# Stick-breaking attention: the causal mask added in the score banks by the tensor engine, every tile weighed by the vector engine alone

## The reference, cut to what matters

```
z = einsum(q_blk, k_pre) * scale                       # 128 queries x (i+1)*128 keys
strict = k_pos[None, :] < q_pos[:, None]
log_rest = where(strict, log_sigmoid(-z), 0.0)
suffix = cumsum(log_rest, reverse=True) - log_rest
a = where(strict, exp(log_sigmoid(z) + suffix), 0.0)
out = einsum(a, v_pre)
```

## Time and profile before

| what | value |
|---|---|
| median of three runs | 2162.31 us |
| the profiled execution: time, span | 2162.35 us, 2160.6 us |
| PE, DVE, ACT, POOL busy over the span | 93%, 66%, 42%, 33% |
| stick-breaking stage | about 898 to 1085 us |
| mean granted PE clock | 0.965 |

### The profile page before, as it was taken

How to read it: one execution, slowest core, us unless ns; L and a number is a source line. 1 busy time by engine, 2 the same in 40 slices (tenths; PEclk the granted TensorE clock), 3 DMA queues, 4 the chain that set the end, 5 groups by cost and what they waited for, 6 DMA issues and landing times. The chain is left out here.

```text
span 2160.6 us, 26117 instructions
## 1 busy us (share of the span) xinstructions
PE 2015.9 (93%) x9585; PEld 1679.5 (78%) x9585; DVE 1428.6 (66%) x1921; ACT 904.2 (42%) x1606; POOL 723.4 (33%) x602
## 2 busy tenths in 40 slices
PE   4899999999999999877889999994999999999997
PEld 3688888887887689666778888883888888887886
DVE  7756556559798532599955565567656565569896
ACT  6443443434445212566633444443443433334443
POOL 3655545530003021388711100124645555520000
PEclk7899999999999999899899999996999999999999
DMA  3222223244300221432134432230223222264201
GB/s 118 73 83 69 88 83 93 78 179 170 138 20 6 87 89 59 108 78 59 48 91 126 136 88 59 60 108 0 79 83 93 79 82 87 75 239 151 78 1 79
DMA packets 217496, 190.21 MB, mean 88 GB/s; under 512 B 7532, under 2 KB 173976, under 8 KB 217368
## 3 DMA queue, kind: packets, MB, share of 16 engines
q1 hardware_dynamic: 217280, 188.51, 28.2%
q10 hardware_dynamic: 88, 0.02, 0.0%
HBM read 152.85 MB, written 35.65 MB: 87 GB/s over the span
## 5 line engine op out<-in xcount | busy, mean ns | idle before, releaser
L1731 DVE TENSOR_TENSOR w_lo<-st,w_hi 128x512 fp32r<-128x512 f32 x176 | 192.7, 1095 | 200.6 <-ACT w_hi L1321 200.4
L928 PE MATMUL ps<-T_hi,w_lo 128*128 128x512 f32 x704 | 278.4, 395 | 48.4 <-DVE T_lo L1731 47.7
L929 PE MATMUL ps<-T_lo,w_hi 128*128 128x512 f32 x704 | 276.6, 393 | 0.0
L930 PE MATMUL ps<-T_hi,w_hi 128*128 128x512 f32 x704 | 276.4, 393 | 0.0
L928 PE MATMUL ps<-tr_hi,sr_lo 128*128 128x512 f32 x616 | 242.6, 394 | 5.1 <-DVE xT L1920 2.7
L930 PE MATMUL ps<-tr_hi,sr_hi 128*128 128x512 f32 x616 | 240.5, 390 | 0.0
L929 PE MATMUL ps<-tr_lo,sr_hi 128*128 128x512 f32 x616 | 240.3, 390 | 0.0
L928 PE MATMUL ps<-B_hi,w_lo 128*128 128x512 f32 x528 | 207.7, 393 | 8.5 <-DVE w_lo L1731 6.1
L929 PE MATMUL ps<-B_lo,w_hi 128*128 128x512 f32 x528 | 207.3, 393 | 0.0
L930 PE MATMUL ps<-B_hi,w_hi 128*128 128x512 f32 x528 | 207.1, 392 | 0.0
L928 PEld LDWEIGHTS ps<-T_hi,w_lo 128*128 128x128 f32 x704 | 133.6, 190 | 82.6 <-DVE T_lo L1731 33.9
(11 more groups left out here) (236 smaller groups left out, 4752.5 us busy)
## 6 DMA issues: line engine op xcount, KB each, us to landing
gate_raw<-in_ffn_w_gate SPq DMA_DIRECT2D x44, 512.0 KB, 5.3
up_raw<-in_ffn_w_up SPq DMA_DIRECT2D x44, 512.0 KB, 5.1
h_spill<-up_s SPq DMA_DIRECT2D x66, 256.0 KB, 2.0
piece_A<-in_ffn_w_down SPq DMA_DIRECT2D x32, 512.0 KB, 4.5
piece_B<-h_spill SPq DMA_DIRECT2D x32, 512.0 KB, 6.0
wa_raw<-in_w_in SPq DMA_DIRECT2D x16, 512.0 KB, 4.0
wb_raw<-in_w_out SPq DMA_DIRECT2D x16, 512.0 KB, 4.1
wb_raw<-in_mem_w_kv SPq DMA_DIRECT2D x16, 512.0 KB, 3.9
```

Source lines behind the costliest of these rows:

```text
L928: pe.matmul(to, w_lo, m_hi, start=first, stop=False, skip_group_check=joins)
L929: pe.matmul(to, w_hi, m_lo, start=False, stop=False, skip_group_check=joins)
L930: return pe.matmul(to, w_hi, m_hi, start=False, stop=last, skip_group_check=joins)
L1731: return dve.tensor_tensor(to, value, plain(hi), ALU.subtract)
```

## The change

The two selects, POOL's part of the weighing and the semaphores `s_mask` and `s_a_far` go. POOL makes a constant `neg` once, before the stage (0 where the key is before the query, -2^100 elsewhere), and ACT a copy of the identity rounded to fp32r (`ident_r`). PE adds `ident_r` times `neg` to the diagonal block of z between the two score products, so that both sigmoids come out as 1 and 0 there. DVE's scan waits for `rest` alone; DVE weighs the whole tile in one operation after it, waiting for its own scan and for `beta`.

```diff
+        ident_r = at(68, "ident_r", [P, 2 * P], F32R)[:, 0:P]
+        neg = at(69, "neg", [P, 2 * P], F32R)[:, 0:P]
...
+            pool.memset(plain(neg), 0.0).then_inc(s_neg, 1)
+            pool.wait_ge(s_neg, 1)
+            pool.affine_select(out=neg, in_=plain(neg), compare_op=ALU.is_gt, fill=-2.0 ** 100, base=0,
+                               pattern=[[-1, P]], channel_multiplier=1).then_inc(s_neg, 1)
...
-            def mask(m):
-                for nth, (buf, slot, fill) in enumerate(((rest, m % 3, 1.0), (beta, m % 4, 0.0))):
...
-                    pool.wait_ge(s_sig, 2 * m + nth + 1)
-                    pool.affine_select(out=diagonal, in_=diagonal,
...
-            def weigh(m):
-                n = min((tile_at(m)[1] + 1) * P, HALF + 1)
-                pool.wait_ge(s_mask, 2 * (m + 1))
-                pool.wait_ge(s_scan, m + 1)
-                pool.tensor_tensor(beta[:, m % 4, 0:n - 1], beta[:, m % 4, 0:n - 1], rest[:, m % 3, 1:n],
-                                   ALU.mult).then_inc(s_a, 1)
...
                     pe.matmul(z, q_stack[:, h % 2, i * P:(i + 1) * P], k_lo2[:, h % 2, keys],
                               start=True, stop=False)
+                    if keys.stop == n:
+                        pe.matmul(ps[:, z_bank[m][0] + lo // HALF, i * P - lo:n - lo], ident_r, neg,
+                                  start=False, stop=False)
...
                 pe.wait_ge(s_a, m + 1)
-                if weighed(m):
-                    pe.wait_ge(s_a_far, weighed(m))
...
+            pe.wait_ge(s_neg, 2)
+            pe.wait_ge(s_ident_r, 1)
...
+            xn_hi(2, 7)
+            act.wait_ge(p2_step, stepped(0, STEPS - 1))
+            copy(ident_r, ident[:]).then_inc(s_ident_r, 1)
...
                         act.wait_ge(s_a, s - 2)
-                        if weighed(s - 3):
-                            act.wait_ge(s_a_far, weighed(s - 3))
...
-                dve.wait_ge(s_mask, 2 * (m + 1))
+                dve.wait_ge(s_sig, 2 * m + 1)
                 dve.tensor_tensor_scan(r[:, ::-1], r[:, ::-1], r[:, ::-1], 1.0, ALU.mult,
                                        ALU.bypass).then_inc(s_scan, 1)
-                if n > HALF:
-                    dve.wait_ge(s_scan, m + 1)
-                    dve.tensor_tensor(beta[:, m % 4, HALF:n - 1], beta[:, m % 4, HALF:n - 1],
-                                      rest[:, m % 3, HALF + 1:n], ALU.mult).then_inc(s_a_far, 1)
+                dve.wait_ge(s_scan, m + 1)
+                dve.wait_ge(s_sig, 2 * (m + 1))
+                dve.tensor_tensor(beta[:, m % 4, 0:n - 1], beta[:, m % 4, 0:n - 1],
+                                  rest[:, m % 3, 1:n], ALU.mult).then_inc(s_a, 1)
```

More of the change, by code:

```diff
@@ L386, in layer_program @@
         s_stack = [sem("s_stack0"), sem("s_stack1")]
-        s_z, s_sig, s_mask, s_scan = sem("s_z"), sem("s_sig"), sem("s_mask"), sem("s_scan")
-        s_a, s_a_far = sem("s_a"), sem("s_a_far")
+        s_z, s_sig, s_scan = sem("s_z"), sem("s_sig"), sem("s_scan")
+        s_neg, s_ident_r = sem("s_neg"), sem("s_ident_r")
+        s_a = sem("s_a")
         s_aT_ps, s_aT_hi, s_aT = sem("s_aT_ps"), sem("s_aT_hi"), sem("s_aT")
@@ L576, in layer_program @@
         assert all(end <= 4 for _, end in z_bank)
-        def weighed(m):
-            return sum(tile_at(k)[1] >= 4 for k in range(m + 1))
         def turns(m):
@@ L890, in _ @@
                         ins.then_inc(s_wsum, 1)
-            def mask(m):
-                i = tile_at(m)[1]
-                for nth, (buf, slot, fill) in enumerate(((rest, m % 3, 1.0), (beta, m % 4, 0.0))):
-                    diagonal = buf[:, slot, i * P:(i + 1) * P]
-                    pool.wait_ge(s_sig, 2 * m + nth + 1)
-                    pool.affine_select(out=diagonal, in_=diagonal,
-                                       compare_op=ALU.is_gt, fill=fill, base=0, pattern=[[-1, P]],
-                                       channel_multiplier=1).then_inc(s_mask, 1)
-            def weigh(m):
-                n = min((tile_at(m)[1] + 1) * P, HALF + 1)
-                pool.wait_ge(s_mask, 2 * (m + 1))
-                pool.wait_ge(s_scan, m + 1)
-                pool.tensor_tensor(beta[:, m % 4, 0:n - 1], beta[:, m % 4, 0:n - 1], rest[:, m % 3, 1:n],
-                                   ALU.mult).then_inc(s_a, 1)
[L911 to L915, removed]
             for q in range(4, 8):
@@ L1521, in _ @@
             norm_std(3)
-            for c in (7,):
-                xn_hi(2, c)
+            xn_hi(2, 7)
+            act.wait_ge(p2_step, stepped(0, STEPS - 1))
+            copy(ident_r, ident[:]).then_inc(s_ident_r, 1)
             def pool_hi_part(k):
```

## The result

The changed kernel takes 2168.05 us (median of nine runs, 2167.44 to 2170.05), the kernel before 2161.35 us on the same chips (nine runs, 2157.27 to 2162.58): a ratio of 1.0036, 95% interval 1.0026 to 1.0046. It is slower by 5.6 to 9.9 us. The forecast was 2171.0 us in a range of 2165 to 2179.5, slower by 8.7.

A forecast was written before the change was run, and what follows sets the result against it. DVE's queue was taken to bound the stick-breaking stage. A head: -1.94 + 4.22 - 1.0 - 0.2 = +1.08 us; 8 heads +8.6, second wait +0.6, smaller gaps -0.5: +8.7 on 2162.35, 2171.0 us, range 2165 to 2179.5.

The forecast's parts named there:

- DVE bounds the stage: Stick-breaking stage: DVE's queue sets a head's length, 23.02 us, of which about 1.0 us is waits.
- What the scans lose to POOL, 1.94 us a head: DVE's scans: time lost taking turns with POOL, 15.5 us in the stage, all taken off with POOL silent.
- What the weighing adds, 4.22 us a head: DVE's queue: new operations in four short tiles, longer ones in four long, plus their starts; 33.8 us in the stage.
- The waits that go, 1.0 and 0.2 us a head: DVE's waits for ACT's aT_hi vanish, 1.0 us a head, with the overlap lost at each, 0.2 us.
- The gaps that stay: DVE's act_lo of odd heads, writing partitions 64 and up: 0.25 us at each of 16, 4.0 us, before and after.
- DVE's few smaller gaps close, -0.5: DVE's queue: smaller gaps of 0.1 to 0.2 us a head partly close, -0.5 us.
- The second wait, 0.01 us each: DVE's weighing waits for scan and beta: 0.01 us for each of 64, 0.6 us.
- The sum: Whole kernel: +1.08 us a head, +8.6 for 8 heads, +0.6 second wait, -0.5 smaller gaps: +8.7 us.
- The waits that stay: Rival: PE or ACT late again, DVE keeps 1.2 us a head of waits: +18.3, 2180.7 us; chance 0.17.
- The scan's fixed 0.145 us as a hand-over between DVE and POOL: Rival: with POOL silent it falls away in 64 scans and 64 weighings, 18.6 us: 2152 us; chance 0.08.
- The contention from something else: Rival: not POOL but ACT's writes or PE's reads stretched the scans; up to 15.5 us more, 2186; chance 0.04.
- All small gaps closing: Rival: all of DVE's small gaps close, those of odd heads too: +4.2 us, 2166.5; chance 0.12.

The follow-up runs named there:

- no_mask: The changed kernel without PE's 64 products that add the mask, the mask being left out of the computation: 2168.29 us.
- swap_after: The changed kernel with odd heads processed before even ones and their act_hi and act_lo copied for all 128 partitions: 2162.09 us.
- pool_reads: The changed kernel, with POOL doing two selects and a product per tile on buffers of its own: 2194.55 us.
- pool_writes: The changed kernel, with POOL writing three memsets of 128x1024 per tile, which read nothing: 2168.39 us.
- weigh_dve: Against the kernel before, DVE weighs every tile in one operation; POOL still makes the two selects: 2171.96 us.
- swap_before: The kernel before with only odd heads first and their act_hi and act_lo copied for all 128 partitions: 2157.82 us.
- masks_pe: Mask on PE as in the changed kernel, but POOL keeps weighing the first 512 keys and DVE the rest: 2152.04 us.
- the other two swap kernels: Odd heads first with full act_hi and act_lo copies, on the changed kernel (swap_after, 2162.09 us) and on masks_pe (2149.56 us).
- near256: masks_pe with odd heads first and full copies, and POOL weighing only 256 keys of a head's four long tiles: 2150.44 us.

## Why the prediction was right

**DVE bounds the stage.** Right; no_mask, which takes work from PE alone, moves nothing, and swap_after, which closes gaps in DVE's queue, makes the stage 4.3 us shorter.

**What the scans lose to POOL, 1.94 us a head.** Measured 1.96. That it was POOL's reads and not its writes is shown by pool_reads against pool_writes. The price of the undisturbed scans, from a line through two of them, held within 0.01 us for every shape.

**What the weighing adds, 4.22 us a head.** The eight operations of a head now last 6.06 us where four lasted 1.98: 4.09, and 4 x 0.03 for their starts: 4.21.

**The waits that go, 1.0 and 0.2 us a head.** Right: 8.1 us became 0.3. What is left of a head's growth, -1.96 + 4.21 less the measured 1.11, is 1.14 us for the two terms together. weigh_dve shows that the waits went with POOL's weighing and not with its selects; how much of them went because DVE's own steps grew longer isn't shown.

**The gaps that stay.** Right in kind, too small: 0.25 us at each act_lo of an odd head, where the traces show 0.36, as I hadn't counted the next aT_lo. In the sum for the change this term had no weight, as it stands in both kernels, where DVE doesn't wait anyway; in the stage 2.7 us of it could be won before and 4.3 after. The term "DVE's few smaller gaps close, -0.5" couldn't be seen.

**The second wait, 0.01 us each.** The weighing starts 0.03 to 0.04 us behind its scan, as the far one did before with one wait; the 0.6 us aren't there. That the sum came out so close is in part luck: this term of +0.6 and the -0.5 of the smaller gaps, neither of which showed, cancel.

**The sum.** A head was to grow by 1.08 us and grew by 1.11. From the first 896-key scan to the stage's last act_lo (its start at 1088.43 before, 1095.27 after) the stage takes 195.58 us against 186.75: +8.83, for +8.7 forecast. The whole grew by less, 6.7 us by the medians. In the profiled executions 2.0 us of the difference lie before the first 896-key scan (901.68 and 899.69). There PE's granted clock was 0.93 from 700 to 750 us in the profile of before and 1.00 in that of the changed kernel, and also 1.00 in that of swap_before, whose program is the same up to the loads of q and k and whose 896-key scan starts at 899.68. The rows of before, changed and swap_before, with the granted clock behind the five engines' busy times:

```profile
700.00:750.00 50.00, 44.70 (x179) 33.80 (x178) 27.12 (x43) 13.28 (x21) 5.26 (x7) 0.93 0.24 79
```
```profile
700.00:750.00 50.00, 43.65 (x187) 33.47 (x186) 27.57 (x43) 13.81 (x23) 6.13 (x9) 1.00 0.26 84
```
```profile
700.00:750.00 50.00, 43.68 (x187) 33.57 (x186) 27.60 (x43) 13.64 (x22) 5.73 (x7) 1.00 0.26 84
```

So the profile on which I summed had 2 us that its kernel doesn't always pay; 2162.35 us was about 1 us above the median of nine runs as well. The changed kernel's stretch behind the stage was 1.2 us shorter, and here too the granted clock differs. From 24 to 36 us behind the last act_lo PE is busy all the time; in before, the changed kernel and masks_pe:

```profile
1112.43:1124.43 12.00, 12.00 (x47) 9.74 (x46) 4.94 (x10) 3.10 (x6) 1.81 (x1) 0.86 0.12 36
```
```profile
1119.27:1131.27 12.00, 12.00 (x49) 9.75 (x48) 4.13 (x7) 3.26 (x5) 1.80 (x1) 0.90 0.15 44
```
```profile
1103.61:1115.61 12.00, 12.00 (x54) 9.94 (x53) 5.24 (x8) 3.98 (x6) 2.35 (x2) 1.00 0.15 44
```

Over all profiles the clock there goes with the time behind the stage: 0.84 to 0.86 in before, swap_before and weigh_dve (1071.7 to 1072.2 us), 0.90 to 0.91 in the changed kernel, pool_writes and no_mask (1070.9 to 1071.1), 0.99 to 1.00 in masks_pe, the other two swap kernels, near256 and pool_reads (1069.6 to 1070.0). What made the clock differ stays open. The 2 us that weigh_dve gains outside the stage against before are those ahead of it (899.6 against 901.7).

**The rivals.** The waits that stay: refuted in the changed kernel, true of masks_pe. The scan's fixed 0.145 us as a hand-over between DVE and POOL: refuted, 2280 ns at 1024 keys is the line's value with POOL silent. The contention from something else: refuted by pool_writes and by the scans. All small gaps closing: not by this change.

## What to carry to other kernels

Where two engines take turns at a resource, moving work from the one to the bounding other pays back only the part that it had stood behind: here 1.96 us of held scans and about 1.1 us of waits a head against 4.2 us of added work. Ask of each half of such a change which of the engines has the time: the mask, moved to an engine with time to spare, made a head 0.8 us shorter; the weighing, moved to the engine that bounds, made it 1.9 us longer (masks_pe against the changed kernel). Before you sum, and before you give an edit in one stage the whole difference of two times, check in the rows outside the stage whether the two executions had the same granted clock there: of the 9.6 us of masks_pe the stage shows 5.4.

## What the runs showed of the hardware that I had not expected

- Where a DVE operation on partitions 64 to 127 stands among operations that start at partition 0, three are late, by 0.11 to 0.13 us each: itself, the next one and the next that reads PSUM. Where the data allow it, 256 columns on all 128 partitions cost the same 0.33 us start to start as on 64, and starting at partition 0 takes the gaps away (4.3 us of the changed kernel's stage for 15 of them).
- Of two operations that a scan's end releases on two engines, DVE's own came first: the far weighing began 0.03 us behind the scan, POOL's lasted 1.40 and 1.53 us instead of 1.09. So DVE's queue paid nothing at that place. Of the 7 us by which masks_pe beat the time that I had taken, this order can explain at most the part in the stage: about 3.3 us, by 22.19 us a head against 22.6 in the middle of my range.
